# Two hybrid transformer blocks on one core: a residual with tokens on partitions, and block-1 feed-forwards and output projections with the activations stationary

## What is computed

```python
def first_block(x, ...):                       # DEPTH = 2
    for l in range(DEPTH):
        x = x + 0.5 * swiglu(rms_norm(x, norm_ffn1[l]), ...)      # D_FF = 2816
        x = x + hybrid_mixer(rms_norm(x, norm_mix[l]), ...)
        x = x + 0.5 * swiglu(rms_norm(x, norm_ffn2[l]), ...)
    return rms_norm(x, norm_final)

def swiglu(x, w_gate, w_up, w_down):
    return (silu(x @ w_gate) * (x @ w_up)) @ w_down

def second_block(x, ...):
    for l in range(DEPTH):
        h = rms_norm_2(x, norm_mix_pre[l])
        ...                                     # four branches, gates
        x = x + rms_norm_2(mix, norm_mix_post[l])
        hf = rms_norm_2(x, norm_ffn_pre[l])
        u = causal_depthwise_conv(hf @ ffn_w_up[l], ...)
        gate, val = split(u, 2)
        f = (gelu(gate) * val) @ ffn_w_down[l]
        x = x + rms_norm_2(f, norm_ffn_post[l])
    return x
```

## Time and profile before

| | |
|---|---|
| median of three runs | 2424.51 us |
| span of the profiled execution | 2426.1 us |
| TensorE matmul busy | 2276.7 us, 94% |
| TensorE weight loads busy | 2184.7 us, 90% (beside the matmuls) |
| VectorE busy | 1539.9 us, 63% |
| ScalarE busy | 1063.6 us, 44% |
| GpSimd busy | 489.7 us, 20% |
| mean granted TensorE clock | 0.964 of 2.4 GHz |
| memory read | 363.7 MB, 150 GB/s over the span |

### The profile page before, as it was taken

One profiled execution on the slowest core, in us unless ns is written; L12 is line 12 of the kernel. 1 busy time (PEld: TensorE's weight loads), 2 busy tenths in 40 slices (PEclk: granted clock), 3 DMA queues, 4 the chain that ended last, 5 costly groups with the idle time before them and its releaser, 6 DMA issues.

```text
span 2426.1 us, 44954 instructions
## 1 busy us (share of the span) xinstructions
PE 2276.7 (94%) x17786; PEld 2184.7 (90%) x17786; DVE 1539.9 (63%) x1745; ACT 1063.6 (44%) x1233; POOL 489.7 (20%) x340
## 2 busy tenths in 40 slices
PE   6999999999899999999899988989979998898998
PEld 6999989999899998999898887889979888788997
DVE  5556556555545655654568885567665888656766
ACT  4334345434443435543432544455452254444554
POOL 1002311000100321100124343211012334321100
PEclk8999999999999999999998999999999899999999
DMA  6555434555455543465533433346554343334652
GB/s 218 173 190 167 147 106 155 184 179 190 142 189 179 167 140 105 154 195 189 182 117 113 138 122 103 106 140 208 178 159 122 121 129 118 105 106 141 205 186 76
DMA packets 285231, 366.67 MB, mean 151 GB/s; under 512 B 9970, under 2 KB 257954, under 8 KB 284834
## 3 DMA queue, kind: packets, MB, share of 16 engines
q1 hardware_dynamic: 280064, 359.49, 46.1%
q10 hardware_dynamic: 5026, 5.28, 0.7%
HBM read 363.69 MB, written 1.05 MB: 150 GB/s over the span
## 4 chain that ended last, share of the span: by engine, by line
PE 71%; issue 12%; DVE 8%; POOL 4%; ACT 3%; ACTq 1%; DVEq 0%; DMA 0%; POOLq 0%
PE ps L540 21%; PE ps L542 21%; PE ps L541 21%; POOL wlo L1499 3%; DVE sq L2039 1%; PE ps L586 1%; PE ps L587 1%; PE ps L585 1%; DVE wlo L1544 1%; POOL arena L1520 1%; DVE rstd L1555 1%; ACT whi L1077 1%; PE ps L724 1%; PE ps L826 1%; PE ps L698 0%
## 5 line engine op out<-in xcount | busy, mean ns | idle before, releaser
L540 PE MATMUL ps<-hhi,whi 128*128 128x256 f32 x3792 | 1099.7, 290 | 56.6 <-DVE hlo L1550 41.6
L541 PE MATMUL ps<-hlo,whi 128*128 128x256 f32 x3792 | 1081.8, 285 | 0.0
L542 PE MATMUL ps<-hhi,wlo 128*128 128x256 f32 x3792 | 1081.4, 285 | 0.0
L1544 DVE TENSOR_TENSOR wlo<-raw,whi 128x2048 fp32r<-128x2048 f32 (+2 forms) x314 | 715.0, 2279 | 434.1 <-ACT whi L1077 434.1
L1077 ACT ACTIVATE whi<-raw 128x2048 fp32r<-128x2048 f32 x350 | 656.2, 1881 | 704.0 <-PE ps L542 605.5
L540 PEld LDWEIGHTS ps<-hhi,whi 128*128 128x128 f32 x3792 | 736.2, 194 | 74.0 <-issue 67.3
L541 PEld LDWEIGHTS ps<-hlo,whi 128*128 128x128 f32 x3792 | 736.4, 194 | 3.7 <-issue 3.4
L542 PEld LDWEIGHTS ps<-hhi,wlo 128*128 128x128 f32 x3792 | 735.5, 194 | 0.0
L540 PE MATMUL ps<-hidhi,whi 128*128 128x256 f32 x1056 | 296.4, 281 | 1.4 <-DVE hidlo L1812 1.4
L541 PE MATMUL ps<-hidlo,whi 128*128 128x256 f32 x1056 | 295.0, 279 | 0.0
L542 PE MATMUL ps<-hidhi,wlo 128*128 128x256 f32 x1056 | 295.0, 279 | 0.0
(11 more groups left out here) (247 smaller groups left out, 2604.2 us busy)
## 6 DMA issues: line engine op xcount, KB each, us to landing
raw<-in_ffn_w_up SPq DMA_DIRECT2D x88, 1024.0 KB, 5.2
raw<-in_w_in SPq DMA_DIRECT2D x68, 1024.0 KB, 5.1
raw<-in_ffn_w_down SPq DMA_DIRECT2D x66, 1024.0 KB, 5.0
raw<-in_ffn_w_gate SPq DMA_DIRECT2D x44, 1024.0 KB, 5.3
raw<-in_w_gate SPq DMA_DIRECT2D x32, 1024.0 KB, 5.5
raw<-in_w_branch SPq DMA_DIRECT2D x16, 1024.0 KB, 5.0
raw<-in_nsa_cmp_w SPq DMA_DIRECT2D x8, 1024.0 KB, 5.4
raw<-in_w_out SPq DMA_DIRECT2D x6, 1024.0 KB, 5.0
```

The costliest lines, as they stand in the source:

```text
L540: pe.matmul(o, w_hi, m_hi, start=start, stop=False, skip_group_check=True)
L541: pe.matmul(o, w_hi, m_lo, start=False, stop=False, skip_group_check=True)
L542: return pe.matmul(o, w_lo, m_hi, start=False, stop=stop, skip_group_check=True)
L1544: dve.tensor_tensor(wlo[:, slot, 0:n], raw[:, slot, 0:n], whi[:, slot, 0:n].bitcast(F32), ALU.subtract) \
```

## The change

The residual becomes `xt`, with tokens on partitions (two tiles of 128 tokens by 1024 features), from the load of x to the store of the result.

- A norm is now finished before its product. For each token tile: ScalarE squares two halves of 512 with an accumulated sum, VectorE adds the two sums, ScalarE takes the root, VectorE the reciprocal and scales x by it and by the gain (loaded as a row on all partitions) to `htok`; TensorE turns it in eight transposes, ScalarE copies the high part, VectorE subtracts the low part. Mixers and block-2 feed-forwards wait for all of h (`enter`); block-1 feed-forwards start with the first token tile. Products are no longer multiplied by `rstd`; GpSimd's sums, the `ones` matmuls and the zero matmuls go.
- Block-1 feed-forwards have six blocks of hidden features (384, 384, 512, 512, 512, 512). The activations are stationary and 384 or 512 weight columns move. Hidden values come out with tokens on partitions and are turned by TensorE (step T), one block later, to be stationary in the down product.
- Down products of both blocks and all output projections go through `out_rows`: stationary activations, 512 output features moving, result in four banks (token tile, half).
- Hardware loops are written out. Parameters that stay columns are loaded after x and turned between block 1 and block 2. The result is stored straight from `xt`. A root of one column at the end of each feed-forward makes ScalarE load its table early.

The diff, cut to its core:

```diff
+FW = (384, 384, 512, 512, 512, 512)
+def ffn1_steps():
+    for b in range(NB):
+        yield ("G", b, 0)
+        if b:
+            yield ("T", b - 1, 0)
+        yield ("G", b, 1)
+        if 0 < b < NB - 1:
+            yield from (("D", b - 1, 0), ("D", b - 1, 1))
+        yield from (("U", b, 0), ("U", b, 1))
+    yield ("D", NB - 2, 0)
+    yield ("T", NB - 1, 0)
+    yield from (("D", NB - 2, 1), ("D", NB - 1, 0), ("D", NB - 1, 1))
...
+            def turn_h(p, t):
+                for n in range(2):
+                    pe.wait_ge(h_tok, 4 * p + 2 * t + n + 1)
+                    for c in range(4):
+                        last = pe.transpose(acc(t, n)[:, c * P:(c + 1) * P], htok[:, t, (4 * n + c) * P:(4 * n + c + 1) * P], ident)
+                    last.then_inc(h_turned, 1)
+            def enter(p):
+                for t in range(TT):
+                    turn_h(p, t)
+                pe.wait_ge(h_ready, 4 * p + 4)
+            def mm3x(o, x_hi, x_lo, w_hi, w_lo, start, stop):
+                pe.matmul(o, x_hi, w_hi, start=start, stop=False)
+                pe.matmul(o, x_hi, w_lo, start=False, stop=False)
+                return pe.matmul(o, x_lo, w_hi, start=False, stop=stop)
+            def out_rows(slot, n, x_hi, x_lo, first, final):
+                for t in range(TT):
+                    for hf in range(2):
+                        for i in range(n):
+                            w = slice(i * D + hf * HALF, i * D + hf * HALF + HALF)
+                            last = mm3x(acc(t, hf), x_hi[:, i, tok(t)], x_lo[:, i, tok(t)], whi[:, slot, w], wlo[:, slot, w],
+                                        first and i == 0, final and i == n - 1)
...
+                def columns(i, t):
+                    kind, b, part = F1[i]
+                    w, s = FW[b], slot(i)
+                    o = bank((0 if kind == "G" else 2) + t, 0, w)
+                    for k in range(4):
+                        kk = 4 * part + k
+                        last = mm3x(o, hhi[:, kk, tok(t)], hlo[:, kk, tok(t)], whi[:, s, k * w:(k + 1) * w],
+                                    wlo[:, s, k * w:(k + 1) * w], kk == 0, kk == KC - 1)
+                    return last
+                def turn_hidden(b):
+                    for t in range(TT):
+                        pe.wait_ge(f1_hid, 2 * fb + t + 1)
+                        for c in range(FW[b] // P):
+                            last = pe.transpose(bank(2 + t, c * P, P), hid_tok1[:, t, c * P:(c + 1) * P], ident)
+                        last.then_inc(f1_turned, 1)
+                turn_h(p, 0)
+                for i in range(2):
+                    ready(i)
+                    pe.wait_ge(h_ready, 4 * p + i + 1)
+                    last = columns(i, 0)
+                last.then_inc(gate_acc, 1)
+                turn_h(p, 1)
+                for i in range(2):
+                    pe.wait_ge(h_ready, 4 * p + 2 + i + 1)
+                    columns(i, 1).then_inc(used[slot(i)], 1)
...
+            def x_squares(st, event, t):
+                for n in range(2):
+                    act.activation(htok[:, t, half(n)], xt[:, t, half(n)], ACT.Square, accum_out=ss[:, 2 * t + n:2 * t + n + 1]) \
+                        .then_inc(sq_done, 1)
+            def enter_norm(p, event):
+                for t in range(TT):
+                    x_squares(st_pre(p), event, t)
+                    std_of(st_pre(p), t)
+                    h_high(p, t)
+                if p + 1 < N_PRE:
+                    act.wait_ge(h_tok, 4 * p + 4)
+                    act.dma_start(gain_pre, PRE_GAINS[p + 1]).then_inc(pre_in, 16)
...
+            def update_and_norm(a, slot, u, scale, p):
+                update(a, slot, u, scale, 0)
+                rstd_of(st_pre(p), 0)
+                normed(p, 0)
+                update(a, slot, u, scale, 1)
+                h_low(p, 0)
+                rstd_of(st_pre(p), 1)
+                normed(p, 1)
+                h_low(p, 1)
+            def post_update(m):
+                dve.wait_ge(post_in, 16 * (m + 2))
+                for t in range(TT):
+                    rstd_of(st_post(m), t)
+                    scaled(st_post(m), t, acc)
+                    for n in range(2):
+                        dve.wait_ge(scaled_tok, 4 * m + 2 * t + n + 1)
+                        dve.tensor_tensor(xt[:, t, half(n)], xt[:, t, half(n)], post_tok[:, t, half(n)], ALU.add).then_inc(x_up, 1)
...
-                        dve.scalar_tensor_tensor(qk[:, c:c + 2, :], out2, scale, rstd_over(2), ALU.mult, ALU.mult) \
-                            .then_inc(unit_taken, 1)
+                        dve.tensor_scalar(qk[:, c:c + 2, :], out2, scale, None, ALU.mult).then_inc(unit_taken, 1)
```

## The result

| | before | after |
|---|---|---|
| median of six runs each, side by side | 2424.84 us | 2434.14 us (2432.8 to 2434.72) |
| ratio after to before | | 1.0037, 95% interval 1.0026 to 1.0049 |
| span of the profiled execution | 2426.1 us | 2432.8 us |
| mean granted TensorE clock | 0.964 | 0.963 |

The forecast was 2396 with a range of 2365 to 2432. The change makes the kernel slower, and the time lies outside the range, near the rival that gave 2439.

The account below looks back on a forecast made before the run. TensorE's matmul pace plus waits at norm boundaries bound the kernel. Matmul streams save 82.5 us, boundaries add 54.2, net 28.3 off the median 2424.5: 2396 us, range 2365 to 2432.

Parts of the forecast that it names:

- part 1: Matmuls of both blocks: 0.217 us per 512-column and 0.164 per 384-column fp32r matmul, 82.5 us saved.
- The toll belongs to the fp32r instruction: Rival on wide fp32r matmuls: each keeps 13.7 ns, +42.5 us, 2439, slower than before; chance 0.09.
- matmul streams: TensorE's feed-forward and output projection matmuls: wider columns, fewer tolls, no zero or statistics matmuls; 82.5 us saved.
- second stops and half clock inside stages: After mixer and feed-forward entries: 3.0 us for half clock, 2.3 for tile 1's transposes and copies; regrouped +21.8 us.
- into a mixer, twice: Block 1 mixer entries: TensorE waits 10.9 us for all of h, against 0.4 now; +21.0 us regrouped.
- into a feed-forward after a mixer, twice: Block 1 feed-forward entries: tile 0 starts 5.5 us late, plus 1.3 for the root's table; +12.8 us regrouped.
- feed-forward to feed-forward: Block 1, once: 10.9 us against 7.0 + 3.0 now, +0.9; regrouped as -1.5 us.
- start: Kernel start: first matmul at about 19 us instead of 24.3, parameter loads out of the way; regrouped -5.3 us.
- block 2, mixer to feed-forward, twice: Block 2: post norm and pre norm chained, 15.5 us against 8.7 now; +13.6 us.
- end: Kernel end: no turning back or split, 8.3 us from the last matmul instead of 16.5; -8.2 us.
- serial count: Norm boundaries: update, squares, root, scaling, transposes and copies, one token tile after the other, 16.1 us for both.
- What hides the rest: Feed-forwards: splits, silu, copies, turned blocks and DMA fit behind TensorE's matmuls; only 0.4 us of issue for gain_pre loads.

Follow-up runs that it names:

- streams: Both blocks left out, TensorE runs prepared matmul streams alone, then with other engines busy: fp32r 0.2267 us at 512 columns, bf16 0.216, fp32 0.429.
- order: Kernel after with the norm boundaries' steps reordered, tile 1's update starting before tile 0 is scaled, weight split deferred: 2418.4 us (0.9966).
- start: Kernel after with parameter loads issued one at a time in the first feed-forward and ScalarE's root table loaded early: 2425.8 us.
- best_shift: Kernel after with repaired boundaries, late parameter loads, early table loads, hidden tensors moved 32 bytes, 256-column products reading h 64 bytes off the weights: 2373.1 us (0.9788).
- best_shift192: best_shift with the second copy of h 192 bytes off the weights instead of 64: 2372.7 us (0.9782).
- before_shift192: Kernel before with par declared in front of hhi, so hhi and hlo start 192 bytes further modulo 256: 2380.7 us (0.9821).
- triples: Both blocks left out, TensorE alone runs the kernels' matmul triples with h shifted 0 to 224 bytes against the weights: 0.1133 to 0.1200 us at 256 columns.
- order_start_table: Kernel after with the changes of order and start plus an early ScalarE table load in each mixer: 2418.9 us.

## Why the forecast was wrong

The failed step is in part 1: "I take 0.217 us for a 512-column fp32r matmul (the bf16 row) and 0.164 for 384 columns". The sentence before it, "Where the column stream is twice as long as the weight load, most of the toll is gone", read a property of the type as one of the length: its rows were fp32 and bf16, and streams shows that these pay 3 ns at 256 columns as well, while fp32r pays 13.3 ns at 512 (0.2267 us) and at 384. The rival *The toll belongs to the fp32r instruction* was right, with 0.227 as priced, and had a chance of 0.09. The steady toll in thousands of fp32r rows spoke for it, and three rows of other types were no evidence against it. That its 2439 lies only 5 us from the measured 2434 is partly luck. It had the tolls 9 us too small (it knew nothing of the 0.2333 of the down products) and shared the forecast's errors elsewhere: 5 us too little between the stages and 21 too much inside them.

Point by point, in us against the kernel before (the sum's own terms, regrouped into what lies inside a stage and what lies between last and first matmul):

| | forecast | measured |
|---|---|---|
| matmul streams | -82.5 | -31.1 |
| second stops and half clock inside stages | +21.8 | +0.6 |
| into a mixer, twice | +21.0 | +20.3 |
| into a feed-forward after a mixer, twice | +12.8 | +9.8 |
| feed-forward to feed-forward | -1.5 | -3.0 |
| start | -5.3 | +0.4 |
| block 1 to block 2 | 0 | +1.2 |
| block 2, mixer to feed-forward, twice | +13.6 | +15.0 |
| block 2, feed-forward to mixer | 0 | +2.8 |
| end | -8.2 | -9.2 |
| sum (the two spans: +6.7) | -28.3 | +6.8 |

The first line from the paces: a block-1 feed-forward has 384 x 0.2267 + 192 x 0.1733 + 264 x 0.2333 + 44 x 0.109 = 186.7 us instead of the 176.9 that I took, 39.1 for four; the output projections 384 x 0.0097 = 3.7; block 2's down products 528 x 0.0163 = 8.6. That is 51.4 less saved. The gaps are start differences of product matmuls in the two traces. The second line is what the ten stages, from first to last product matmul, leave (30.5 us shorter in all); so it is no measurement of its own, and everything that the first line leaves out inside the stages falls into it.

- *The toll.* 51 us, as above. Of these, 10.6 are the start of the hidden tensors against the weights (0.2333 instead of 0.2267).
- *Inside the stages.* I charged 3 us of half clock at each entry and 2.3 for each second stop. The stops were 1.0 us, and the clock cost less: the feed-forwards after run at 0.99, and one second mixer at 0.96 where both had 0.94 before. 21 us too much; it hid part of the error. That is luck: without it the forecast would have been further off.
- *Boundaries.* The serial count was good to 1 us for mixer entries and to 3 for the others. order shows that it is indeed the order of the small steps: the same steps otherwise arranged take 2.3 to 4.3 us less at each entry into a mixer and each norm of block 2.
- *Start.* The parameter loads were not moved out of the way, as I had read: they are still issued on ScalarE's queue behind x, until 14.3 us, ahead of its first square. That was a misreading of the change: they are waited for later, but issued at the same place. start, with the table load taken ahead as well, gave 8.4 us.
- *What hides the rest.* Right: in the feed-forwards TensorE waits for nothing, the turned blocks cost only their own time, 0.87 us for eight, and DMA at 0.54 to 0.58 held nothing up. A transpose took 0.109 us, as the 0.11 said.

And the gain that was computed for wider streams was not a matter of width alone. With the toll of 13.3 ns in each, 512 columns save one toll for each two matmuls; but 256 columns at another place pay 6.7 ns (0.1133), and 2 x 0.1133 is 0.2267, the best that 512 columns showed anywhere. The gate, up and down streams of a block-1 feed-forward take 186.7 us after with its transposes, 189 before, and 11 x 16.54 = 182 in the kernel before with h at another place. The change is worth something only with its boundaries repaired: best_shift at 2373 and best_shift192 at 2373, 2.1% and 2.2% faster than the kernel before, and 0.3% faster than before_shift192, whose boundaries were left as they are.

## What to carry to other kernels

Take the pace of a matmul from rows of the very type that the change will run; if the trace has none at the new width, let a stream of some fifty alone decide, before the layout is changed for it. When a stream of fp32r matmuls is slower than its columns, compare where the stationary and the moving tile start modulo 256 bytes and try other places: moving one declaration was worth 1.6% of the kernel before, four times what this change cost. Time the program for each, since the pace of a place alone did not foretell the kernel's time (2381 and 2373 where 2340 to 2360 and 2345 to 2350 were expected). Where a norm becomes a chain between two products, start the second tile's chain before the first one's is finished, and put nothing that is needed later ahead of it.

## What the runs showed of the hardware

- An fp32r matmul carries a toll beside its columns that fp32 and bf16 (3 ns) do not: 13.3 ns at 512, 384 and 256 columns (0.2267, 0.1733 and 0.1200 us) when both tiles start alike modulo 256 bytes, with other engines idle or busy, with new tiles and banks or always the same. For fp32 the 3 ns are those of a record with two passes (0.2158 us at 256 columns, 0.429 at 512).
- With other starts it is 16 to 25 ns at 512 columns (0.2289 to 0.2383) and 6.7 to 13.3 at 256 (0.1133 to 0.1200), and at 256 the same shift took 0.1178 or 0.1167 in triples depending on the stream before it, and 0.1178 or 0.1133 in two layers of before_shift192. No simple rule fits all of them: both tiles shifted by 16 bytes took 0.2300 at 512 columns.
- At half clock the 384-column fp32r matmuls of the kernel after start 0.320 us apart, just their columns at 1.2 GHz: no toll there.
- Transposes of fp32 128x128 tiles start 0.109 us apart in a run (TensorE at the full clock) and 0.214 apart at half clock.
- The granted clock of block 2's mixer was 0.96 in its first layer and 0.94 in its second in the kernel after (377 and 382 us), the other way round in order, and 0.94 in both in order_start_table.
